# Two token-row projections move behind the last attention scores, and the first block's head transposes gather behind the last step

## What is computed

```python
proj = h @ w_in[l]                       # split into q, k, v, gates, latents, retention q/k/v/gate
o_nsa = nsa_mixer(...)                   # 6 heads: compressed, selected and window attention, gated
o_mla = mla_mixer(...)                   # 5 heads of causal attention from latents
o_ret = retention_mixer(ret_q, ret_k, ret_v, ret_gate, ...)   # 5 heads
mixed = concatenate([o_nsa, o_mla, o_ret])
x = x + mixed @ w_out[l]

def retention_mixer(...):                # its end is what the change rearranges
    o = chunkwise_retention(q, k, v)
    mu = mean(o); var = mean(square(o - mu))
    o = (o - mu) * rsqrt(var + EPS) * gn_gain
    return silu(gate) * o
```

## Time and profile before

| | us |
|---|---|
| median of 3 runs (1633.3 to 1636.15) | 1635.92 |
| the profiled execution | 1631.49 |
| its span | 1629.7 |
| PE busy | 1517.5 (93%) |
| DVE busy | 1111.0 (68%) |
| ACT busy | 783.2 (48%) |

### The profile page before, as it was taken

The page is one execution under the profiler, slowest core; times in us unless marked ns, Lnnn a source line. Parts: engine busy times, 40 slices in busy tenths (PEclk is TensorE's granted clock), DMA queues, the critical chain, the costliest instruction groups (busy, mean ns, idle before and its releaser), DMA issues.

```text
span 1629.7 us, 28708 instructions
## 1 busy us (share of the span) xinstructions
PE 1517.5 (93%) x11878; PEld 1469.1 (90%) x11878; DVE 1111.0 (68%) x1860; ACT 783.2 (48%) x1367; POOL 59.6 (4%) x61
## 2 busy tenths in 40 slices
PE   4899789999899879999999988999989998889999
PEld 4788689999888778999899988999989998889999
DVE  5848578787657767788888557666557854766653
ACT  5534357733435436753455544544445554344442
POOL 0000000000000000000002011000000300200000
PEclk9979789999989978999999999999999999999999
DMA  7223149899421435889644434454544443435552
GB/s 276 86 104 130 52 147 329 290 346 337 168 95 49 159 103 218 301 332 350 244 171 161 156 135 155 146 191 182 181 155 155 156 156 129 157 134 201 182 181 78
DMA packets 41889, 296.50 MB, mean 182 GB/s; under 512 B 4641, under 2 KB 4769, under 8 KB 6305
## 3 DMA queue, kind: packets, MB, share of 16 engines
q1 hardware_dynamic: 41184, 293.31, 49.3%
q10 hardware_dynamic: 576, 1.37, 0.2%
HBM read 293.61 MB, written 1.05 MB: 181 GB/s over the span
## 4 chain that ended last, share of the span: by engine, by line
PE 72%; DVE 14%; DMA 6%; ACT 5%; issue 2%; POOL 1%; ACTq 0%; SPq 0%; DVEq 0%
PE acc L743 21%; PE acc L744 21%; PE acc L745 21%; DMA ring<-stream 6%; DVE wL L1564 5%; ACT wH L1251 3%; PE acc L918 1%; DVE ring L1554 1%; PE ps_t L855 1%; POOL region L2181 1%; PE acc L825 1%; PE acc L926 1%; PE ps_s L842 1%; POOL region L2182 1%; PE ps_o L865 0%
## 5 line engine op out<-in xcount | busy, mean ns | idle before, releaser
L1564 DVE TENSOR_TENSOR wL<-ring,wH 128x1024 fp32r<-128x1024 f32 x444 | 547.7, 1241 | 303.1 <-ACT wH L1251 298.8
L743 PE MATMUL acc<-hH,wH 128*128 128x256 f32 x2368 | 697.1, 294 | 35.7 <-DVE hL L1573 20.5
L744 PE MATMUL acc<-hL,wH 128*128 128x256 f32 x2368 | 681.4, 288 | 0.0
L745 PE MATMUL acc<-hH,wL 128*128 128x256 f32 x2368 | 680.7, 287 | 0.0
L1251 ACT ACTIVATE wH<-ring 128x1024 fp32r<-128x1024 f32 x444 | 462.3, 1050 | 243.2 <-PE acc L745 133.1
L743 PEld LDWEIGHTS acc<-hH,wH 128*128 128x128 f32 x2368 | 466.8, 197 | 49.3 <-issue 39.5
L744 PEld LDWEIGHTS acc<-hL,wH 128*128 128x128 f32 x2368 | 467.2, 197 | 3.6 <-issue 2.9
L745 PEld LDWEIGHTS acc<-hH,wL 128*128 128x128 f32 x2368 | 466.0, 197 | 0.0
L743 PE MATMUL acc<-aH,wH 128*128 128x256 f32 x864 | 244.8, 283 | 0.8 <-DVE wL L1564 0.8
L744 PE MATMUL acc<-aL,wH 128*128 128x256 f32 x864 | 244.5, 283 | 0.0
L745 PE MATMUL acc<-aH,wL 128*128 128x256 f32 x864 | 244.5, 283 | 0.0
(11 more groups left out here) (298 smaller groups left out, 1549.8 us busy)
## 6 DMA issues: line engine op xcount, KB each, us to landing
ring<-stream SPq DMA_DIRECT2D x276, 1024.0 KB, 4.9
cst<-consts SPq DMA_DIRECT2D x1, 1411.0 KB, 15.0
x<-xin SPq DMA_DIRECT2D x4, 256.0 KB, 5.5
out<-x SPq DMA_DIRECT2D x4, 256.0 KB, 4.1
onc<-once ACTq DMA_DIRECT2D x1, 516.0 KB, 9.6
v1all<-vec ACTq DMA_DIRECT2D x1, 371.0 KB, 7.2
v2all<-vec SPq DMA_DIRECT2D x1, 330.0 KB, 19.2
nv<-pos ACTq DMA_DIRECT2D x1, 256.0 KB, 4.3
```

The lines of the kernel that those rows point to most:

```text
L743: pe.matmul(out, w[0], y[0], start=first, stop=False)
L744: pe.matmul(out, w[0], y[1], start=False, stop=False)
L745: return pe.matmul(out, w[1], y[0], start=False, stop=last)
L1564: TTN(wL[:, n % SPLIT, :], ring[:, g % RING, half * UNIT:(half + 1) * UNIT], wH[:, n % SPLIT, :].bitcast(F32), ALU.subtract).then_inc(lo_r ...
```

## The change

`FILL1` gets two empty entries, so `tm30` and `tm31` move from slots 14 and 15 to slots 16 and 17. All of `mt0` to `mt4` stand in slot 18. `fed_by`, which counts what has been read before a slot, follows from the list: units 26 and 27 (`wo2`, `wo3`) are fed in slot 18 rather than 16. Group norm's statistics move from slot 16 to 15, the gain is multiplied onto the normed output rather than onto the gate product, and the gate product and the last product stand in slot 18. ACT's tanh follows `tm31` to slot 17 and so comes behind the root of slot 16.

```diff
-FILL1 = ["tm10", "tm11", "kc", "q2", "kw", "vc", "kpe", "rqa", "rka", "rqb", "rkb", "r4", "tm20", "tm21", "tm30", "tm31"]
+FILL1 = ["tm10", "tm11", "kc", "q2", "kw", "vc", "kpe", "rqa", "rka", "rqb", "rkb", "r4", "tm20", "tm21", None, None, "tm30", "tm31"]
...
-        16: ["mt0", "mt1"], 17: ["mt2"], 18: ["mt3", "mt4"]}
+        18: ["mt0", "mt1", "mt2", "mt3", "mt4"]}
...
-                    if i == 16:
+                    if i == 15:
...
-                        dve.wait_ge(gexp, L * 2 + 2)
-                        link(STT(gx_, gx_, 1.0, tokm[:, :, RG:RG + 320], ALU.add, ALU.mult))
                     if i == 17:
-                        link(TTN(gx_, gx_, V1(L, "gn").unsqueeze(1).to_broadcast([P, TT, 320]), ALU.mult))
                         dve.wait_ge(gn_y, L + 1)
                         refine(0, None, gnst[:, 2, :], gnst[:, 3, :], gnst[:, 4, :], gnst[:, 5, :])
                         link(TTN(o10, o10, bg(gnst[:, 5, :]), ALU.mult))
+                        link(TTN(ro_all(0).rearrange("p (t f) -> p t f", t=TT), ro_all(0).rearrange("p (t f) -> p t f", t=TT),
+                                 V1(L, "gn").unsqueeze(1).to_broadcast([P, TT, 320]), ALU.mult))
+                    if i == 18:
+                        dve.wait_ge(gexp, L * 2 + 2)
+                        link(STT(gx_, gx_, 1.0, tokm[:, :, RG:RG + 320], ALU.add, ALU.mult))
                         link(STT(mixed[:, :, 704:1024], ro_all(0).rearrange("p (t f) -> p t f", t=TT), 0.5, gx_,
                                  ALU.mult, ALU.mult))
```

## The result

The changed kernel is slower: 1646.4 us median of 7 runs against 1634.8 us of 7, a ratio of the means of 1.0078 (95% interval 1.0055 to 1.0102). I had forecast 1632.0. The profiled execution took 1643.9 us with a span of 1642.0.

A forecast was written before the change was run, and what follows sets the result against it. PE, busy 93% of the span, was taken to bound the kernel by products. An earlier `wo0` gains 2.0 us per layer, 4.0 in all: 1635.9 becomes 1631.9, stated as 1632.0; range 1629.0 to 1636.5.

The forecast's parts named there:

- the sum of the prediction: `wo0` starts at 191.2 in place of 193.15 us: 2.0 us gained per layer, 4.0 in all.
- The gap itself: Slot 14: PE idle for 1.9 us, 166.0 to 167.85, until DVE drains the bank that `rs4` needs.
- the cover of the units: Slots 16 and 17: `tm30` and `tm31` run beside DVE's work, `tm30` covered by only 0.35 us; uncovered, each up to 2.74.
- the third load: Before the next norm's root: an added table load hidden by a 2.34 us wait, taken as nothing; at worst 1.28 per layer.
- the switch: ACT's table switch around root and tanh: 1.3 us each; a rival with 2.7 us gave 1638.1, chance 0.03.
- ACT as the late one in slot 18: Slot 18: ACT's chain through root, table load, tanh and feeding ends about 0.6 us later than DVE's own.
- the slower rival: Clock falls in slot 14's gap, stays down over both units: layer some 7.5 us slower, 1641.4 with one layer, chance 0.07.
- three signs of being wrong: Clock 0.50 between 168 and 175 us; third load holding up the next norm's root; DVE, not ACT, late in slot 18.
- The step on PE's clock behind the gap: Slot 14: whether the clock falls after PE's idle 1.9 us was called unknown; a fall was not taken as likeliest.
- the fall: Slot 14's gap: clock falls in one layer or both, gain 2.5 or 1.0 in all, 1633.4 to 1634.9, chance 0.27.
- such a piece loses about 1.7: Behind slot 14's gap: a stretch at 1.2 GHz loses about 1.7 us, less 0.25 of DVE's wait: 1.5 of 2.0.

The follow-up runs named there:

- gap filled: The changed kernel with 16 matmuls of 256 columns that compute nothing on PE in front of `rs4`: 1630.9 us, ratio 0.9995 to the kernel before.
- filled_no_tanh: The gap filled kernel with the retention gate's tanh replaced by a plain scaling, so two table loads per layer go: 1628.8 us, ratio 0.9983 to before.
- wide_units: The changed kernel with `tm30` and `tm31` multiplied over all 256 columns in place of 146: 1634.1 us, ratio 1.0009 to the kernel before.
- held pair: held_narrow and held_wide, the kernel before with an added PE wait in slot 14: 1667.4 us and 1645.5 us.
- half filled: The changed kernel with 8 matmuls of 256 columns, in place of 16, in front of `rs4`: ratio 0.9967 to the kernel before.
- `rs4` first: The changed kernel with `ro2`, `ro3` and `rs4` placed before `co0` and `co1` in slot 14: 1628.1 us, ratio 0.9967 to the kernel before.
- held_narrow: The kernel before with one PE wait added at the head of slot 14, units 146 columns wide: 1667.4 us, ratio 1.0213 to before.
- held_wide: held_narrow with `tm30` and `tm31` over all 256 columns: 1645.5 us, ratio 1.0071 to the kernel before.

## Why the prediction was wrong

The forecast had one step at a time for DVE. Counted from its feeding in slot 14, in us:

| step | before | forecast | changed | gap filled |
|---|---|---|---|---|
| scores of head 15 | 9.5 | 6.2 | 7.2 | 6.4 |
| statistics | 16.9 | 8.1 | 10.5 | 8.2 |
| scores of head 16 | 15.4 | 11.8 | 16.8 | 11.9 |
| output of head 15 | 22.3 | 16.1 | 25.6 | 16.0 |
| last product | 24.9 | 22.8 | 31.8 | 22.8 |
| `wo0` | 29.75 | 27.8 | 36.6 | 27.6 |

- **What held.** Every step, once the clock was up: with the gap filled the forecast is off by 0.2 us at most, and the layer gains 2.16 us where I had 2.0. That is the sum of the prediction, shown for a kernel in which the wait is filled, not for the changed one. The gap itself was forecast at 1.9 us and was 1.91, though for a wrong reason: the bank of `rs4` was the one of `co0` before as well. With the gap filled these came out too: the cover of the units, the third load hidden by a wait (it ends at 214.19 us and the root waits for PE until 214.82), the switch at 1.3 us and not 2.7, and ACT as the late one in slot 18 by about 0.6 (measured 0.6 by `filled_no_tanh`). In the changed kernel itself the units were not covered: DVE waited 2.46 and 6.59 us for them, as the slower rival said. Nor was ACT the late one in slot 18: DVE began to feed 0.17 us behind its own last step (187.87). So two of the three signs of being wrong that the prediction names were seen, the clock at 0.50 between 168 and 175 us and this one.
- **What failed first.** The step on PE's clock behind the gap. I had the fall at 0.27 + 0.07 and took two rows for it, 1.84 us with a fall and 2.49 without. In the 2.49 us row dense products of 256 columns stand on both sides. In the 1.84 us row they stand only ahead of the wait, and behind it the attention's matmuls, most of them of 128, 64 and 30 columns. That is nearer to `rs4`, which has products of 64 columns just ahead of it and the attention's behind. I took the bounds as even. That the work around a wait decides is my reading of these rows and is not shown: in one and the same place, waits of 1.97 and 1.95 us did both (45.84 and 46.51, above).
- **The larger error** is how long it stays down. I priced the fall as one piece of 3.3 us ("such a piece loses about 1.7") and gave the case where it stays down over both units 0.07. In the changed kernel it was down from 164.7 to 202.3 us, 37.5 us, in the first layer and as long in the second. I had read the row behind 472.31 only up to 476.6. In the kernel before, the clock that fell there stays at 0.50 up to 486.9 us, 13.7 us in all, with PE busy throughout. The end of it in the trace of the kernel before, columns as in the earlier trace rows:

```profile
483.49:486.90 3.41, 3.41 (x16) 3.23 (x16) 0.85 (x2) 0.00 (x0) 0.00 (x0) 0.50 0.96 399
```

- Most of the work there is narrow (30 columns, line 918, from 474.99 to 481.8), and the clock is back 5.1 us after products of 256 columns begin (481.79). `tm30` and `tm31` are 146 wide. At the half clock PE is busy 4.00 of 4 us with them and the clock does not come back, neither within them nor between them; `wide_units` and the held pair show that the width decides whether it is back within the unit. The rival's price was about right: 7.5 us per layer forecast, 6.8 measured to `wo0` and 7.0 and 7.2 to the next root. Its chance wasn't.
- **The range** ended at 1636.5, because it left this rival out.
- By the traces the three kernels with the whole change and without the fall win 4.3 us (filled, half filled) and 5.7 us (`rs4` first) in their two layers, which would be ratios of 0.9974 and 0.9965. Measured are 0.9995, 0.9967 and 0.9967; for the first, 0.9974 lies just outside the measured interval (0.9975 at its lower end). Why that one shows less in the whole kernel I did not settle.

The Trainium skill, "TensorE: Matmul & The Clock Gate", section "HAM oscillation — how this bites in real kernels", describes a kernel whose bursts between waits each start at the slow clock, and advises padding thin products. The runs agree with both (the 21 us behind the wait in the changed kernel at 0.50, and 6.0 us per layer back by padding), and add that here the two thin units did not end the slow state although PE was busy without a break (4.00 of 4 us).

## What to carry to other kernels

Work that PE does early, ahead of a step that DVE holds back, also keeps its clock up; before you move it away, look at what PE will wait for in its place (here a PSUM bank that DVE drains at its own time: the turn was the same as before, PE only came to it earlier) and price the idle time with the clock down over all that follows, not over one stretch. Judge whether the clock returns by rows of the same shape of matmul, and follow such a row until the clock is back, not for one stretch: dense and wide is not dense and narrow. Widening a product into padding can be almost free (0.12 us a matmul in place of 0.11 at the full clock, 0.21 for both at the half). If a move costs more than its steps add up to, fill the new gap with matmuls that compute nothing as a test; then remove the wait itself.

## What the hardware showed that I had not expected

- Matmuls of 146 columns kept the full clock when it was up (slots 14 and 15 of the kernel before: 0.11 us each, clock 1.00) and did not raise it when it was down (0.21 us each, PE busy 4.00 of 4 us, clock 0.50). In the changed kernel PE was busy without a break for 21 us behind the wait (164.11 to 185.1), the two units and other products of 64 to 256 columns between them, and in `held_narrow` for 29 us (163.3 to 192.4), and the clock stayed at the half. It was there for 37.5 and 51.2 us in all, waits and the start of `w_out` included.
- Those of 256 columns raised it within 2.6 us of their start in `wide_units` (175.3 to 177.9) and cost the same 0.21 us each at the half clock. How long they need differs: 4.2 us in `held_wide`, 3.6 in `w_out` of the kernel before, 6.0 in that of the changed kernel.
- An idle time of 1.9 us in front of `rs4` was followed by the fall in both layers; 0.9 us, with eight wide matmuls ahead of it, was not. Elsewhere waits of 1.66 and of 1.95 to 1.97 us were followed by a fall in one layer or execution and by none in another.
- A table switch on ACT costs 1.28 us and nothing more, in each load that I followed (in the changed kernel 183.62 to 184.91), and it runs ahead of the wait of the instruction that needs it (in the kernel before the load ends at 182.34 and the root waits for DVE until 184.16).
